# Expert stage of a two-block transformer: four experts share the stationary columns of one product, in plain fp32 straight from the weight ring

## The reference, cut to what matters

```python
logits = (xt @ w_router + b_router).astype(jnp.float32)
top_val, top_idx = lax.top_k(logits, TOP_K)             # 32 experts, top 4
gates = jax.nn.softmax(top_val, axis=-1)
...
def expert_block(args):
    tok, g, e = args
    xb = xt[tok]
    hb = clamped_swiglu(xb @ w_gu[e] + b_gu[e])         # 1024 -> 2 x 1024
    yb = hb @ w_down[e] + b_down[e]                     # 1024 -> 1024
    return yb * g[:, None].astype(yb.dtype)
```

## Time and profile before

| Engine | busy us | share of span | instructions |
|---|---|---|---|
| PE | 2607.5 | 94% | 16642 |
| PEld | 2086.0 | 75% | 16642 |
| DVE | 1847.9 | 66% | 1789 |
| ACT | 1466.4 | 53% | 1628 |
| POOL | 630.1 | 23% | 243 |

### The profile page before, as it was taken

One profiled execution on the slowest core, in us unless ns is written; L12 is line 12 of the kernel. 1 busy time (PEld: TensorE's weight loads), 2 busy tenths in 40 slices (PEclk: granted clock), 3 DMA queues, 4 the chain that ended last, 5 costly groups with the idle time before them and its releaser, 6 DMA issues. The chain is left out here.

```text
span 2788.0 us, 41851 instructions
## 1 busy us (share of the span) xinstructions
PE 2607.5 (94%) x16642; PEld 2086.0 (75%) x16642; DVE 1847.9 (66%) x1789; ACT 1466.4 (53%) x1628; POOL 630.1 (23%) x243
## 2 busy tenths in 40 slices
PE   8989987999999999999999989979988699899998
PEld 6668755788888888888888757757677577788887
DVE  6575246899999999999999943546745433422233
ACT  4344334677777777777777742336645322522222
POOL 0003002244444444444444320001132000000000
PEclk9989998999999999999999989989999899999999
DMA  5344224899999999999999853431000323122220
GB/s 209 120 157 138 85 89 181 332 383 382 382 382 381 384 382 383 382 382 382 382 383 382 352 210 128 152 109 68 20 33 4 119 87 134 48 98 99 91 100 36
DMA packets 114571, 595.70 MB, mean 214 GB/s; under 512 B 12144, under 2 KB 13936, under 8 KB 69808
## 3 DMA queue, kind: packets, MB, share of 16 engines
q1 hardware_dynamic: 98944, 539.07, 49.7%
q0 software_dynamic: 7056, 25.69, 3.0%
q10 hardware_dynamic: 8448, 29.17, 2.7%
HBM read 568.72 MB, written 25.17 MB: 213 GB/s over the span
## 5 line engine op out<-in xcount | busy, mean ns | idle before, releaser
L1352 DVE TENSOR_TENSOR weights_low<-weight_ring,weights_high 128x2048 fp32r<-128x2048 f32 x384 | 865.1, 2284 | 56.0 <-ACT weights_high L1298 55.8
L1298 ACT CAST weights_high<-weight_ring 128x2048 fp32r<-128x2048 f32 x384 | 726.8, 1909 | 180.9 <-PE psum L1207 146.9
L1167 POOL TENSOR_SCALAR rank_onehot<-iota,members 128x128 bf16<-128x128 f32 x132 | 442.0, 3358 | 1.0 <-issue 0.2
L358 DVE TENSOR_TENSOR w_low<-weight_ring,w_high 128x2048 fp32r<-128x2048 f32 (+1 forms) x92 | 213.7, 2324 | 326.0 <-ACT w_high L353 325.7
L353 ACT CAST w_high<-weight_ring 128x2048 fp32r<-128x2048 f32 (+1 forms) x88 | 166.6, 1893 | 291.6 <-PE psum L392 146.3
L1207 PE MATMUL psum<-weights_high,expert_x_high 128*128 128x512 f32 x1024 | 279.0, 394 | 2.9 <-DVE expert_x_low L1356 2.9
L1207 PE MATMUL psum<-weights_low,expert_x_high 128*128 128x512 f32 x1024 | 274.7, 390 | 0.0
L1207 PE MATMUL psum<-weights_high,expert_x_low 128*128 128x512 f32 x1024 | 274.5, 390 | 0.0
L1161 POOL DMA_INDIRECT expert_x<-hidden,index x33 | 89.7, 2718 | 776.4 <-DVE index L1347 593.6
L1207 PEld LDWEIGHTS psum<-weights_low,expert_x_high 128*128 128x128 f32 x1024 | 193.0, 189 | 40.5
L1207 PEld LDWEIGHTS psum<-weights_high,expert_x_low 128*128 128x128 f32 x1024 | 192.8, 188 | 40.2
(11 more groups left out here) (549 smaller groups left out, 4515.4 us busy)
## 6 DMA issues: line engine op xcount, KB each, us to landing
weight_ring<-in_w_gu SPq DMA_DIRECT2D x256, 1024.0 KB, 8.9
weight_ring<-in_w_down SPq DMA_DIRECT2D x128, 1024.0 KB, 8.9
weight_ring<-in_w_in SPq DMA_DIRECT2D x35, 1024.0 KB, 4.8
weight_ring<-in_w_ada SPq DMA_DIRECT2D x24, 1024.0 KB, 4.9
weight_ring<-in_w_ffn_in SPq DMA_DIRECT2D x22, 1024.0 KB, 4.9
expert_table<-expert_y ACTq DMA_DIRECT2D x32, 512.0 KB, 9.2
weight_ring<-in_w_ffn_out SPq DMA_DIRECT2D x11, 1024.0 KB, 4.9
weight_ring<-in_w_out SPq DMA_DIRECT2D x8, 1024.0 KB, 5.6
```

What stands on the lines that cost most here:

```text
L358: self.m.nc.vector.tensor_tensor(low, w, high.bitcast(F32), ALU.subtract).then_inc(self.ready.sem, 1)
L1167: last = nc.gpsimd.tensor_scalar(oc[:, t, :], iota[:, :], members[:, t, e], None, ALU.is_equal)
L1298: nc.scalar.copy(high[:, n % 4, :], slot(n)).then_inc(rounded.sem, 1)
L1352: V.tensor_tensor(low[:, n % 4, :], slot(n), high[:, n % 4, :].bitcast(F32), ALU.subtract).then_inc(ready.sem, 1)
```

## The change

Four experts form a group (EG), and CAP goes from 128 to NR x ROUND = 3 x 32 = 96. A stationary operand of 128 columns is now 32 token rows of each of four experts, and each expert's 32 columns are multiplied with that expert's weights by a product of its own, into its own 32 partitions of a PSUM bank; four such products (`tile`) fill a bank, and there are three rounds of tokens and two halves of 512 columns, so six banks. The products are plain fp32 from the ring slots; the rounding on ACT, the rest on DVE and their buffers are gone. A ring unit is now [128 rows, 2 experts, 1024 columns], in runs of 4 KB, and two units (four experts) make one step of 128 rows; a group has 24 steps: gate, then up, then down. The slots of a step are given back by the first product of the next step. Gate, up and down use the same six banks one after another. The six bias products of gate and of up follow each bank's last tile. One-hots of ranks are made on DVE. Three gathers and three stores of 512 KB serve a group.

```diff
-CAP = 128
+EG = 4
+ROUND = P // EG
+NR = 3
+CAP = NR * ROUND
...
+GROUPS = E // EG
+PAIRS = 3 * KD
...
+def group_units(dram, e, first=0):
+    out = []
+    for q in range(first, PAIRS):
+        c, k = q // KD, q % KD
+        for h in range(2):
+            if c < 2:
+                src = dram["w_gu"][e(2 * h), k * P:(k + 1) * P, c * D:(c + 1) * D]
+            else:
+                src = dram["w_down"][e(2 * h), k * P:(k + 1) * P, :]
+            out.append(src.rearrange("e p n -> p e n"))
+    return out
...
-    high, low = sb("weights_high", [P, 4, SLOT], F32R), sb("weights_low", [P, 4, SLOT], F32R)
...
+            with sp.Fori(1, LAST) as e:
+                for q, src in enumerate(group_units(m.dram, lambda i: bass.ds(e * EG + i, 2))):
+                    load(U0 + q, src, U0 + q - NSLOT + 1, e * LOOP)
...
+            def tile(w, xs, j, c, k, stop=False):
+                for a in range(EG):
+                    q = slice(ROUND * a, ROUND * a + ROUND)
+                    ins = T.matmul(bank(j, c)[q, :], xs[:, k, j, q], w[a // 2][:, a % 2, half(c)], start=(k == 0), stop=stop)
+                    if a == 0:
+                        first = ins
+                return first, ins
...
+            def group(e, at_start=False, at_end=False):
+                for k in range(KD):
+                    w = landed(k, e)
+                    if k == 2 and not at_end:
+                        list_rows(e)
...
+                    for o, (j, c) in enumerate(rows_first):
...
+                        first, _ = tile(w, xT, j, c, k)
+                        if o == 0:
+                            first.then_inc(ring.used, 1 if at_start and k == 0 else 2)
+                        if k == KD - 1:
+                            with_bias(j, c, 0, gate_done)
...
+                        if 1 <= k < 3 and o % NR == 0 and 2 * (k - 1) + o // NR < NR:
+                            turn_h(NR + 2 * (k - 1) + o // NR, e)
+                        if k >= 4 and o % NR == 0 and 2 * (k - 4) + o // NR < B and not at_end:
+                            turn_x(2 * (k - 4) + o // NR, e + 1, (e + 1) * B)
+                        if k == 0:
+                            pe.wait_ge(up_freed.sem, e * B + up_freed.at(NR * c + j + 1))
...
-            def round_weights(n, e=None):
-                nc.scalar.copy(high[:, n % 4, :], slot(n)).then_inc(rounded.sem, 1)
...
-            def rest_of_weights(n, e=None):
-                V.tensor_tensor(low[:, n % 4, :], slot(n), high[:, n % 4, :].bitcast(F32), ALU.subtract).then_inc(ready.sem, 1)
...
+def mark_group(nc, oc, iota, members, e):
+    for j in range(NR):
+        last = nc.vector.tensor_tensor(oc[:, j, :, :].rearrange("p t (a i) -> p t a i", a=EG),
...
-    R0, R1 = CAP // P, S // P
+    R0, R1 = 0, math.ceil((S - CAP) / P)
```

More of the change, by code:

```diff
@@ L1109, in experts @@
[L1109 to L1115, removed]
@@ L1196, in parts @@
[L1196 to L1209, removed]
@@ L1211, in gate_up_bias @@
[L1211 to L1218, removed]
-                    last = T.matmul(ps[bank][:, 0:2], oc[:, t, :], tok[:, 2 * t:2 * t + 2], start=(t == 0), stop=(t == NT - 1))
-                last.then_inc(listed.sem, 1)
[L1222 to L1226, removed]
-                    for k in range(2):
-                        for i, (xs, w) in enumerate(parts(h_high[:, 2 * q + k, :], h_low[:, 2 * q + k, :], n0 + q)):
-                            for c in range(2):
-                                ins = T.matmul(ps[4 + c][:, :], xs, w[:, k * D + c * 512:k * D + (c + 1) * 512],
-                                               start=(q == 0 and k == 0 and i == 0), stop=(q == DNN - 1 and k == 1 and i == 2))
-                                if k == 0 and c == 0 and i == 0:
-                                    ring.release(ins)
-                ins.then_inc(down_done.sem, 1)
@@ L1289, in _ @@
+            for i in range(B):
+                turn_x(i, 0, 0, later=False)
+            group(0, at_start=True)
+            with pe.Fori(1, LAST) as e:
+                group(e)
+            group(LAST, at_end=True)
+            pe.wait_ge(y_copied.sem, y_copied.at(B * GROUPS))
+            pe.sem_inc(ring.used, 1)
+            ring.next_use = U0 + N
         @block.scalar
         def _(act):
-            def round_weights(n, e=None):
-                landed, used = 16 * (n // NSLOT + 1), n - 3
-                if e is not None:
-                    landed, used = (e - 1) * (16 * LOOP // NSLOT) + landed, (e - 1) * LOOP + used
-                act.wait_ge(ring.landed[n % NSLOT], landed)
-                act.wait_ge(ring.used, used)
-                nc.scalar.copy(high[:, n % 4, :], slot(n)).then_inc(rounded.sem, 1)
@@ L1340, in _ @@
+            copy_x(0)
+            group(0)
+            with act.Fori(1, LAST) as e:
+                group(e)
+            group(LAST, at_end=True)
+            for j in range(NR):
+                act.wait_ge(y_stored[j].sem, y_stored[j].at(16 * GROUPS))
         @block.vector
@@ new lines, in _ @@
+            mark(slice(0, EG))
+            mark_ranks(slice(EG, 2 * EG))
+            group(0, at_start=True)
+            with dve.Fori(1, LAST) as e:
+                group(e)
+            group(LAST, at_end=True)
+    n = B * GROUPS
+    index_ready.end(LAST), onehot.end(GROUPS), listed.end(LAST), sel_ready.end(GROUPS)
+    for z in (x_turned, x_copied, gate_done, gate_ready, sig_done, gate_scaled, up_done, up_freed, h_ready, h_turned, h_copied, down_done, y_copied):
+        z.end(n)
+    for j in range(NR):
+        gathered[j].end(16 * GROUPS), y_stored[j].end(16 * GROUPS)
```

396 lines of the change are left out of this document (186 added, 210 removed).

## The result

The changed kernel takes 2901.7 us in the median (2898.68 to 2902.61, four runs), the kernel before beside it 2791.9: a ratio of 1.0386, 95% interval 1.0366 to 1.0406. I had forecast 2772, in a range from 2735 to 2820. It is 110 us slower, where I expected 21 less.

What follows compares the result with a forecast made beforehand. PE was taken to bound the kernel, DVE and DMA close behind. A group of 138.3 + 3.3 = 141.6 us against 142.4 saves 6 us over eight, the ends 15.1: 2793.6 - 21 = 2772 us, range 2735 to 2820.

Steps and rivals of the forecast that it cites:

- The products: Expert products on PE: four 32-column products run together, 0.433 us per round of four records, 124.7 us a group.
- The rival of three at a time: Expert products on PE: only three of four run together at 512 columns, 3116 us; incomplete overlap had chance 0.07.
- What stands between them: PE between expert products, per group: biases 2.6 us, turns 4.8, list products 0.7, changes of product width 5.5.
- The sum of 138.3 us a group: PE's own work per group: 124.7 + 2.6 + 4.8 + 0.7 + 5.5 us, against 142.4 before.
- DVE, ACT and POOL: Other engines in the expert stage: no wait counted; one or two us per group if up's last-step cover fails.
- The DMA: Expert-stage loads: 53.5 MB a group at 415 GB/s, 128.9 us, below PE's time; 3.3 us of waiting added.
- 2.0 us of slack: Ring loads: a pair, needed about 9.4 us after its request, lands after 7.4 us on an idle queue.
- The forecast's 3.3 us: PE's waiting per group for loads delayed by bursts: 1.8 us for three stores, 1.5 for the gathers.
- The ends: Start and end of the expert stage: 3.5 us instead of 18.6, 15.1 saved.
- The ring is too shallow: Weight loads: at most two pairs in flight, 383 GB/s, 145.6 us a group, 2804 us; chance 0.25.

Runs made afterwards that it cites:

- e8: Changed kernel with weights laid out in 8 KB runs, eight ring slots and PE's six middle groups written out: 2759.7 us, ratio 0.9894.
- e2: Changed kernel with gate's and up's weights laid out as separate matrices, 4 KB runs without gaps between rows: 2859.2 us, ratio 1.0228.
- e1: Changed kernel with the experts' weights laid out in DRAM in ring-unit order, runs of 8 KB: 2839.3 us, ratio 1.0176.
- e7: Changed kernel with 8 KB runs and eight ring slots together, PE's loop kept: 2793.2 us, ratio 1.0006.
- e5: Changed kernel with eight ring slots instead of six, loads in the same shape: 2832.0 us, ratio 1.0140.
- e6: Changed kernel with PE's six middle groups written out instead of a loop: 2886.3 us, ratio 1.0330.
- e3: Kernel before with its w_gu units loaded in the changed kernel's shape, 4 KB half rows of two experts: 2797.3 us, ratio 1.0033.
- e4: Changed kernel loading only a quarter of the experts' weight bytes, so that no load can bind: 2774.0 us, ratio 0.9935.

## Why the prediction was wrong, by its own steps

**The products: right.** The forecast had rounds of four records in 0.433 us, four at a time. Down's steps of the changed kernel:

```profile
735.89 10.51 PE L1214 MATMUL psum<-weight_ring,expert_hT 128*32 128x512 f32 x96
746.33 0.66 PE L1176 MATMUL psum<-ident,expert_x 128*128 128x128 f32 x4
```

10.44 us for 24 rounds, 0.435. The rival of three at a time (3116 us) is refuted for this kernel. The Trainium skill's figure for three column tiles ("TensorE: Matmul & The Clock Gate", Measured speedup vs the span model), 2.38 times, is not borne out by the four here, which run at four times.

**What stands between them: right.** A bank with its bias product, 0.867 + 0.22 + 0.25 = 1.34 us by the forecast:

```profile
715.19 0.39 PE L1220 MATMUL psum<-bias,sel_gu 96*128 96x512 bf16 x1
715.51 1.06 PE L1214 MATMUL psum<-weight_ring,expert_xT 128*32 128x512 f32 x8
716.51 0.39 PE L1220 MATMUL psum<-bias,sel_gu 96*128 96x512 bf16 x1
```

1.32. The sum of 138.3 us a group is 137.7 by e8. DVE, ACT and POOL: no wait, as forecast.

**The DMA: this step failed.** I took 415 GB/s, a pair in 5.05 us, less than a step's 5.20, and 3.3 us of waiting a group (0 to 7.6). That rested on 2.0 us of slack, from a pair that lands after 7.4 us on an idle queue; one load of w_gu lands 8.7 us after its issue in the median from 632 to 1268 us (down's 6.9). Measured are 355 over busy time, so a pair takes 2.10/0.355 = 5.9 us (6.1 in gate and up), longer than a step; 81.9 + 2.0 + 1.2 = 85.1 us of waits, 10.6 a group; and 6.2 us of lower clock, in one group, behind these and the turn, which the forecast had as nothing. The forecast's 3.3 us stood behind the stores and the gathers, that is, in gate. In the group from 791.3 us PE waits 4.4 us there (3.58 at 804.96, 0.81 at 822.88), and 4.9 in up (2.23 at 848.68, 2.71 at 868.75), where no burst is and the forecast had none. The 415 came from the earlier trace rows, a stretch in which runs of 4 KB were loaded. But those were down's, with no gap between rows. The row held the length of the run and not the distance, which costs twice as much (6 us against 3). And it was measured on a ring with four units of parts behind it, where the queue is full; with PE as the only one that hands slots back, in six slots, the same 4 KB runs without gaps come at 375 (e2).

**The turn of the loop: not in the sum.** 28.3 us in five turns. In the kernel before PE's loop turns some 30 times without a stop (busy for all of 1102.10 us), and the forecast has no term for it. Its body leaves 168 matmul records, the new one 1224.

**The ends: partly right.** From the first product to the last copy it is 1716.87 - 462.57 = 1254.3 us, 17.7 less than 8 x 159.0, where I had 3.5 more than eight groups. Some 9.4 of the 17.7 are stops: eight times the mean would hold 37.7 us of them (28.3 in six groups), and there are 28.3. For the rest, that the last group has no gathers and the first starts with full slots fits, but is not separated. Not in the sum: the 9.5 us behind the stage.

**Where the 113 us are** (2900.8 less 2788.0, profiled): 3.8 before the stage's first product, 96.0 from there to PE's last one (1253.5 against 1157.5), 9.5 behind it, 3.3 in code that did not change. The 21.3 us that a group takes above PE's own work, in the order in which they were taken out: 9.0 with the shape of the loads (e1), 5.4 with the depth of the ring (e7), 5.4 with the turn (e8), and 1.5 is left, the 9.1 us of waits in e8. In another order the shares are others: depth alone gives 9.7 (e5), the turn alone 2.4 (e6). What one repair saves can come back as another's wait.

**The rivals.** "The ring is too shallow" (0.25, 2804 us) had the right sign and the right mechanism, a plain step shorter than its pair; its 383 GB/s, from the same trace, was too fast as well. A chance of 0.28 for slower was too low: every rate in the trace was one of loads with a different address pattern and a deeper buffer, and the range should have had a bound for a rate that no row showed. The Trainium skill's figure for loads from HBM ("DMA: Bandwidth & Descriptors", Where 436 GB/s comes from), about 358 GB/s, is near to what the changed kernel's queue gives. As a limit for this one core it does not agree: e8 holds 385 over 636 us with other addresses for the same bytes, 374 of them loads and gathers (231.45 + 6.29 MB).

## What to carry to other kernels

When a change removes a copy between the ring and the engine that uses the data, count the copy's buffers as part of the ring's depth, and compare a step with the time that its loads take: slower loads that cost 0.3% in the kernel before had their part in a loss of 3.9% here. Which buffer was the cover is argued here and not shown. Take a transfer's rate only from a row with the same address pattern: the same run length, the same distance between runs; and if the distance is a power of two, try the layout with a little padding first. Where several causes delay the same engine, a repair of one shows only part of its worth: e6 alone gave 0.6%, behind the other two 1.1%.

## What the hardware showed that I had not expected

- In the changed kernel, with six slots: half rows of 4 KB at a distance of 8 KB, 355 GB/s over busy time; at 9 or 12 KB 376 and 374; without gaps 375; as runs of 8 KB 387. It is not the shape's number alone: the half rows come at 363 with eight slots (e5) and at 373 in the kernel before (e3), and the 8 KB runs at 394 and 403 in e7 and e8.
- A loop of PE with over 1200 matmul records stands still for 3.3 us at a turn with a light DMA queue (16.7 in five) and for 5.2 to 6.1 with a busy one. Written out, the same code has no such stop. In the 6 us from 774 to 780 the trace has two packets on a queue of kind "instruction"; then the same queue from 632 to 1268 us, and last, in the kernel before, from 500 to 1600:

```profile
q8 instruction: 2, 0.03, 2.0%
```
```profile
q8 instruction: 48, 0.79, 0.5%
```
```profile
q8 instruction: 1, 0.02, 0.0%
```

  So this queue is still during the short loop and busy all along the long one, and each of the five stops has one packet in it. In windows of half a us, that packet moves 2.0 to 3.6 us after the stop's start in the changed kernel and within the first 1.0 us in e4, and PE goes on 3.0 to 3.4 us after the start of that window in all ten. Where the stop is longer, the packet is later. That the stop is the fetch of the loop's first instructions, queued behind loads and stores, fits all of this, but no run separated it from other causes.
- Two rearrangements of loads at the stage's end moved waits to other places and did not shorten the 63.6 us from the last expert product to L397 (68.4 with the loads held back, 63.6 with them moved).
